# Three decode pairs of each attention computed between token tiles of the projections, and the second layer's projections reordered

## What is computed

```python
def diff_attention(q, k, v, lam, q_pos0):             # layer A
    ...
    p = jax.nn.softmax(jnp.where(mask, s, -jnp.inf), axis=-1)
    w = p[:, :, 0] - lam * p[:, :, 1]
    outs.append(jnp.einsum('bhqk,bkhd->bqhd', w.astype(v.dtype), vb))

def stick_breaking_attention(q, k, v, q_pos0):        # layer B
    ...
    log_1m = jnp.where(mask, jax.nn.log_sigmoid(-z), 0.0)
    suffix = lax.cumsum(log_1m, axis=3, reverse=True) - log_1m
    a = jnp.where(mask, jnp.exp(jax.nn.log_sigmoid(z) + suffix), 0.0)
    outs.append(jnp.einsum('bhqk,bkhd->bqhd', a.astype(v.dtype), vb))
```

## Time and profile before

| | |
|---|---|
| median of 3 runs | 1649.18 us (1644.54 to 1650.6) |
| span of the profiled execution | 1647.5 us |
| TensorE busy | 1616.3 us (98%) |
| VectorE busy | 1151.9 us (70%) |
| ScalarE (ACT) busy | 740.6 us (45%) |
| GpSimd (POOL) busy | 145.7 us (9%) |
| DMA | 265.45 MB, mean 161 GB/s |

### The profile page before, as it was taken

One profiled execution on the slowest core, in us unless ns is written; L12 is line 12 of the kernel. 1 busy time (PEld: TensorE's weight loads), 2 busy tenths in 40 slices (PEclk: granted clock), 3 DMA queues, 4 the chain that ended last, 5 costly groups with the idle time before them and its releaser, 6 DMA issues.

```text
span 1647.5 us, 31458 instructions
## 1 busy us (share of the span) xinstructions
PE 1616.3 (98%) x13140; PEld 1483.3 (90%) x13140; DVE 1151.9 (70%) x1605; ACT 740.6 (45%) x1228; POOL 145.7 (9%) x123
## 2 busy tenths in 40 slices
PE   8999999999999999999999999999999999999999
PEld 6888766699999999999999896666999999999999
DVE  5765477668984797488742328989689848974874
ACT  5444366765541344134432215768555413531441
POOL 0000000012210011012000000000122201110110
PEclk9999999999999999999999999999999999999999
DMA  7133899941222122222244358996412221221222
GB/s 286 52 111 132 350 418 418 419 160 52 86 94 103 52 78 103 77 78 78 103 166 140 112 209 360 420 418 288 167 66 89 95 85 52 103 102 53 78 103 90
DMA packets 39596, 265.45 MB, mean 161 GB/s; under 512 B 4256, under 2 KB 4640, under 8 KB 10272
## 3 DMA queue, kind: packets, MB, share of 16 engines
q1 hardware_dynamic: 36720, 252.95, 39.8%
q0 software_dynamic: 2736, 10.49, 1.8%
HBM read 247.69 MB, written 15.73 MB: 160 GB/s over the span
## 4 chain that ended last, share of the span: by engine, by line
PE 85%; DVE 8%; DMA 3%; issue 2%; ACT 2%; SPq 0%; DVEq 0%; ACTq 0%
PE ps L584 30%; PE ps L799 28%; PE ps L268 5%; PE ps L269 4%; PE ps L270 4%; PE ps L1260 2%; PE ps L1319 2%; DVE s_lo L748 2%; PE ps L611 2%; PE ps L1204 2%; DMA kv<-in_v_a 1%; PE ps L1238 1%; DMA xT<-in_v_a 1%; PE ps L1225 1%; DVE pw L1621 1%
## 5 line engine op out<-in xcount | busy, mean ns | idle before, releaser
L230 ACT ACTIVATE w_hi<-w_raw 128x2048 fp32r<-128x2048 f32 x55 | 105.1, 1910 | 190.3 <-PE ps L584 158.5
L246 DVE TENSOR_TENSOR w_lo<-w_raw,w_hi 128x2048 fp32r<-128x2048 f32 x55 | 126.0, 2291 | 71.4 <-ACT w_hi L230 71.4
L744 ACT ACTIVATE s_hi<-t 128x512 fp32r<-128x512 f32 x176 | 109.4, 626 | 144.6 <-PE ps L799 65.8
L799 PE MATMUL ps<-hs_hi,s_hi 128*128 128x320 f32 x528 | 163.8, 310 | 0.0
L799 PE MATMUL ps<-hs_hi,s_lo 128*128 128x320 f32 x528 | 163.2, 309 | 0.0
L799 PE MATMUL ps<-hs_lo,s_hi 128*128 128x320 f32 x528 | 163.1, 309 | 0.0
L584 PE MATMUL ps<-gu_hi,w_hi 128*128 128x320 f32 x692 | 157.9, 309 | 0.2
L584 PE MATMUL ps<-gu_lo,w_hi 128*128 128x320 f32 x692 | 157.7, 309 | 0.0
L584 PE MATMUL ps<-gu_hi,w_lo 128*128 128x320 f32 x692 | 157.6, 309 | 0.0
L748 DVE TENSOR_TENSOR s_lo<-t,s_hi 128x512 fp32r<-128x512 f32 x176 | 132.8, 760 | 5.4 <-ACT s_hi L744 4.6
L268 PE MATMUL ps<-w_hi,h_hi 128*128 128x512 f32 x320 | 126.8, 396 | 8.1 <-DVE h_lo L300 8.1
(11 more groups left out here) (298 smaller groups left out, 3995.9 us busy)
## 6 DMA issues: line engine op xcount, KB each, us to landing
w_raw<-in_w SPq DMA_DIRECT2D x99, 1024.0 KB, 4.8
kv<-in_k_a SPq DMA_DIRECT2D x12, 1024.0 KB, 16.1
kv<-in_v_a SPq DMA_DIRECT2D x12, 1024.0 KB, 16.7
kv<-in_v_s SPq DMA_DIRECT2D x12, 1024.0 KB, 12.6
kv<-in_k_s SPq DMA_DIRECT2D x12, 1024.0 KB, 15.0
xT<-in_k_a SPq DMA_DIRECT2D x8, 1024.0 KB, 17.4
xT<-in_k_s SPq DMA_DIRECT2D x8, 1024.0 KB, 11.7
work<-in_v_a SPq DMA_DIRECT2D x7, 1024.0 KB, 14.9
```

What stands on the lines that cost most here:

```text
L230: nc.scalar.activation(w_hi[s][:, :, :], w_raw[:, s, :, :], ACT.Copy).then_inc(hi_done, 1)
L246: nc.vector.tensor_tensor(w_lo[s][:, :, :], w_raw[:, s, :, :], w_hi[s][:, :, :].bitcast(F32), ALU.subtract).then_inc(lo_done, 1)
L744: nc.scalar.activation(s_hi[i][:, :, :], factor(j % 2, i), ACT.Copy).then_inc(hi_done, 1)
L799: last = nc.tensor.matmul(ps[:, bank[i], 0:HALF], w[:, p, :], m[:, p, :], start=(i < 3 and p == 0 and a == 0), stop=(p == 3 and a == 2), s ...
```

## The change

- `EARLY = 3`: the first three decode pairs of each attention, now sequences 0, 1, 2 with the first half of the heads (`PAIRS` sets the new order of the 16), are computed during the last two units before the slots, in fixed places after token tiles (`pe_early`, `act_early_before`, `act_early`), in banks 5 to 7, one pair after the other, with tiles of their own (`sp_early` in `rows`, `sw_early` in `extra`).
- The slots still number 16, with the same prompt steps; slot i now has pair i + 3, and slots 13, 14 and 15 have none.
- Layer B's units come in the order keys, queries, values, so that the last two units are token units there too. `h_lo` is made anew twice (`low_again`), for the queries in the keys' last unit and for the values in the queries' last unit.
- The ring's order differs: in A 16 pieces have places before the end of the units, in B 14; further loads of SP move among them. `qs` has room for four sequences and lies in `xT`.
- The norm of the decode outputs in layer A (`sub_pe(7)`, `sub_pe(8)`) moves into the last slot.

```diff
-        order = [("qkv", 12, TT, 1), ("oa", 4, 2, 1), *layer(0), ("ks", 4, 2, 1), ("vs", 4, TT, 1), ("qb", 4, 2, 1),
+        order = [("qkv", 12, TT, 1), ("oa", 4, 2, 1), *layer(0), ("ks", 4, 2, 1), ("qb", 4, 2, 1), ("vs", 4, TT, 1),
...
-        RING_A = ("x0 x1 extra work0 work1 raw1 w_hi0 w_lo0", "x0 x1 w_hi1 w_lo1 extra work0 work1 raw1 w_hi0 w_lo0")
-        RING_B = ("x0 x1 extra raw1 w_hi0 w_lo0", "x0 x1 work0 work1 w_hi1 w_lo1 extra raw1 w_hi0 w_lo0")
+        RING_A = ("x0 x1 extra work0 work1 x0 x1 raw1 extra work0 work1 x0 w_hi0 w_lo0 x1 raw1",
+                  "w_hi1 w_lo1 extra work0 work1 x0 w_hi0 w_lo0 x1 raw1")
+        RING_B = ("x0 x1 work0 work1 x0 x1 raw1 work0 work1 x0 x1 raw1 w_hi0 w_lo0",
+                  "w_hi1 w_lo1 extra work0 work1 x0 x1 raw1 w_hi0 w_lo0")
...
+        PAIRS = [(b, 0) for b in range(EARLY)] + [(b, 1) for b in range(EARLY)] + \
+            [(b, g) for b in range(EARLY, DEC_B) for g in range(G)]
...
+            def pe_early(self, unit, t):
+
+                step = (unit, t)
+                if step == (0, 0):
+                    self.pe_s(0)
+                elif step == (0, 2):
+                    self.pe_weights(0)
+                elif step == (0, 3):
+                    self.pe_new(1)
+                    self.pe_v(0)
+                    self.pe_s(1)
+                elif step == (1, 0):
+                    self.pe_o(0)
+                    self.pe_weights(1)
+                elif step == (1, 1):
+                    self.pe_new(2)
+                    self.pe_v(1)
+                    self.pe_s(2)
+                elif step == (1, 3):
+                    self.pe_o(1)
+                    self.pe_weights(2)
+                elif step == (1, 4):
+                    self.pe_ps(0)
+                    self.pe_s(3)
+                    self.pe_v(2)
...
             def pe_a(self, pe):
-                for n in range(N_PAIRS):
-                    k = 2 * n
+                for i in range(N_PAIRS):
+                    k, n = 2 * i, i + EARLY
...
+                    if n + 1 < N_PAIRS:
+                        self.pe_s(n + 1)
+                    if n < N_PAIRS:
+                        self.pe_v(n)
...
+        def low_again(dve, gain, hi, ph, free, done, made=None):
+
+            for t in range(KT):
+                if made is not None:
+                    dve.wait_ge(made, t + 1)
+                dve.wait_ge(*((free, t + 1) if t < KT - 1 else (mm, tiles_before(ph, 0))))
+                nc.vector.scalar_tensor_tensor(h_lo[:, t, :], xT[:, t, :], norms["kv"].g(t, gain),
+                                               hi[:, t, :].bitcast(F32), ALU.mult, ALU.subtract).then_inc(done, 1)
...
-            ta.loads(sp_, slice(3, 5), {"work0": [(qk["stored"], 64), (qk["tr"], 8)]})
+            work_free = [(qk["stored"], 64), (qk["tr"], 8)]
+            ta.loads(sp_, slice(3, 9), {"work0": work_free, "work1": work_free, "raw1": [(lo_done, splits[u_a - 1])]})
             load(u_a, 0)
-            ta.loads(sp_, slice(5, None), {"raw1": [(lo_done, splits[u_a - 1])],
+            ta.loads(sp_, slice(9, None), {"raw1": [(lo_done, splits[u_a - 1])],
                                            "w_hi0": [(mm, tiles_before("qkv", 11))],
                                            "w_hi1": [(mm, tiles_before("oa", 0))]})
...
+            x_free, work_free = [(kept, 16), (mix1["back"], KT)], [(mm, tiles_before("vs", 0))]
+            tb.loads(sp_, slice(0, 4), {"x0": x_free, "x1": x_free, "work0": work_free, "work1": work_free})
+            load(u_v + 3, 1)
+            tb.loads(sp_, slice(4, 9), {"raw1": [(lo_done, splits[u_b - 1])]})
+            load(u_b, 0)
+            tb.loads(sp_, slice(9, None), {"w_hi0": [(mm, tiles_before("vs", 3))],
+                                           "w_hi1": [(mm, tiles_before("ob", 0))],
+                                           "extra": [(tb.s["p"], EARLY)]})
...
             nc.scalar.preload_act_table_set("sigmoid_and_others")
-            tb.act_b(act, "ob", [(kq["stored"], 48)])
+            split_hi(act, "vs", 3, 1)
+            tb.act_early_before(act)
+            act.wait_ge(mm, tiles_before("vs", 3))
+            token_evac(act, "vs", 1, lambda t: v5[:, t, 2 * UC:4 * UC], kq["vev"], lambda t: tb.act_early(act, t))
+            tb.act_b(act, [(mm, tiles_before("ob", 0))], "ob", [(kq["stored"], 48)])
...
-            for j in range(2, 11):
+            for j in range(2, 10):
                 token_unit(pe, "qkv", j, qk["ev"])
-                if j < 10:
-                    qk_transposes(pe, j - 2)
+                qk_transposes(pe, j - 2)
             pe.wait_ge(qk["tev"], 8)
             pe.wait_ge(setup["const"], 1)
-            ta.pe_ps(0)
-            token_unit(pe, "qkv", 11, qk["ev"], between=lambda t: ta.pe_s(0) if t == 1 else None)
+            for j in range(2):
+                token_unit(pe, "qkv", 10 + j, qk["ev"], between=lambda t: ta.pe_early(j, t))
             ta.pe_a(pe)
```

More of the change, by code:

```diff
@@ L456, in first_unit, with token_unit @@
                         last.then_inc(mm, 1)
-        def token_unit(pe, ph, j, ev, free=None, k_done=None, between=None):
+        def token_unit(pe, ph, j, ev, free=None, ready=None, between=None):
             pe.wait_ge(lo_done, split_count(ph, j))
+            if ready is not None:
+                pe.wait_ge(*ready)
             for t in range(TT):
@@ L587, in feature_unit @@
                                 stop=(k == kts - 1 and i == 2), skip_group_check=True)
+                    if k_done is not None and n == 1 and k < kts - 1:
+                        last.then_inc(k_done, 1)
                 last.then_inc(mm, 1)
@@ L1262, in pe_s, with scored, pe_new @@
                     last.then_inc(s["kused"], 1)
-                if 1 not in part:
-                    return
+                if 1 in part and (n == 0 or n >= EARLY):
+                    self.pe_new(n).then_inc(s["s"], 1)
+            def scored(self, eng, n):
+                if 0 < n < EARLY:
+                    eng.wait_ge(self.s["kused"], 2 * n + 2)
+                else:
+                    eng.wait_ge(self.s["s"], 1 if n == 0 else n - EARLY + 2)
+            def pe_new(self, n):
+                pe, s = nc.tensor, self.s
+                b, g = PAIRS[n]
+                q = qs[:, b % 4]
+                pe.wait_ge(s["q"], b + 1)
+                self.wait(pe, s["x"], n)
                 self.wait(pe, s["wn"], n)
                 self.wait(pe, s["o"], n - 1)
+                if n == EARLY:
+                    self.tile_out(pe, 2)
                 for t in range(4):
@@ L1627, in dve_prod, with odd, dve_q @@
                 nc.vector.tensor_tensor(x, x, self.pw[p][:, :, SEQ - n + 1:SEQ + 1], ALU.mult).then_inc(s["pw"], 1)
-            def queries(self, n):
-                return n // G + (2 if self.b and n > 0 else 1)
-            def dve_q(self, b, tiles=slice(0, KT)):
+            def odd(self, n):
+                return sw_early if n < EARLY else sw
+            def dve_q(self, b):
                 s = self.s
-                self.wait(nc.vector, s["s"], 2 * b - 2)
+                if b >= 4:
+                    self.scored(nc.vector, PAIRS.index((b - 4, 1)))
                 new = slice(b * DEC_T, (b + 1) * DEC_T)
@@ L1766, in dve_b_begin, with dve_b @@
+            def dve_b(self, dve, ch, begin, ended, first, stored):
+                nc.vector.memset(sw_early[:, KEYS:KEYS + 4], 1.0)
+                for b in range(4):
+                    self.dve_q(b)
+                for n in range(EARLY):
+                    self.dve_sprod(ch, n)
+                    if n > 0:
+                        self.dve_o(n - 1)
+                    self.dve_wn(n)
+                for w in begin:
+                    dve.wait_ge(*w)
                 nc.vector.memset(pw0[:, :, SEQ:SEQ + 4], 1.0)
-                nc.vector.memset(sw[:, KEYS:KEYS + 4], 1.0)
@@ L1785, in dve_b @@
+                for w in ended:
+                    dve.wait_ge(*w)
+                ch.link(nc.vector.memset(pw1[:, :, SEQ:SEQ + 4], 1.0))
+                for i in range(N_PAIRS):
+                    k, n = 2 * i, i + EARLY
+                    if i % 2 == 1:
                         self.dve_pt(k - 1)
                     self.dve_prod(ch, k + 1, lambda: self.dve_new(n))
-                    if n % 2 == 0 and n + 2 < N_PAIRS:
-                        self.dve_q(n // 2 + 1)
+                    self.dve_next_q(n)
@@ L1800, in dve_b @@
                     dve.wait_ge(*w)
-                self.dve_lo(2)
-                self.dve_o(N_PAIRS - 1)
-                for t in range(3, 6):
+                for t in range(2, 5):
                     self.dve_lo(t)
@@ L1900, in kq_dve @@
                 for n in range(2):
-                    if j == 3 and n == 1 and between is not None:
+                    if j == 3 and n == 1:
                         between()
```

586 lines of the change are left out of this document (320 added, 266 removed).

## The result

The changed kernel takes 1700.3 us (median of four runs, 1697.5 to 1700.7) against 1648.7 before: a ratio of 1.031, interval 1.030 to 1.033. It is 51.6 us slower; 36 were forecast, and the time lies 3 us above the range. The profiled execution has a span of 1698.3 us.

What follows compares the result with a forecast made beforehand. TensorE bounds the projections, loads the end of each attention's pairs, then prompt steps run alone. 1647.5 + 19 (first attention) + 17 (second) = 1683.5 profiled, so 1685 us as median; range 1664 to 1697.

Steps and rivals of the forecast that it cites:

- Added to the units: Units before the slots: a pair costs TensorE 5.3 us; units end at 202.3 in A, near 1014.7 in B.
- The three waits: TensorE in the last units: 1.6 us for copies and 1.8 for query layout in A, 4.0 for it in B.
- the query wait: Second attention, before scores 0: TensorE waits 4.0 us for the query layout that VectorE makes.
- When the loads end: Key and value loads end at 330.4 in A and 1150.3 in B; last value products near 333 and at 1151.7.
- (1): Rival, chance 0.13: loads are not the limit, both stages end by their chains, +10 us each, 1669 us.
- the main case: Forecast, chance 0.72: loads set when each attention's last value products end, the slots without pairs follow; 1685 us.
- the one from 1150.3 to 1151.7: Second attention: loads end at 1150.3, and the last value products follow at 1151.7.
- The tails: From last value products to output product, with slots lacking a pair: 24 us in A, 23 us in B.
- rival (2): Chance 0.06: TensorE's clock falls to half in the three slots without a pair, 6 us on each stage, 1697 us.
- A slot without a pair: Attention slots with prompt steps only: in A 7.0 us against 9.0 with a pair, set by the steps' chain.
- (3): Rival, chance 0.05: slots run at VectorE's busy time, 6.7 us a slot in A, 1639 us.
- (4): Rival, chance 0.04: prompt-only slots take 4.7 us and loads run ahead, 1649 us.

## Why the prediction was right in direction and short in size

**Added to the units: right.** Units ended at 200.6 in A (202.3 forecast, of which 1.1 is that this trace runs 1.1 us earlier at unit 10), and in B 190.1 us after the first unit of the keys, with 189.2 forecast. The three waits were right within 0.4 us. The pieces, not costed inside the units, made TensorE wait 0.9 us in B, and up to 2.5 in other runs. Behind the query wait the clock took another 1.5 us that the sum did not have.

**When the loads end: right in A.** Last value products at 332.4, forecast 333. The forecast that slots can't run ahead of the loads was the right one of (1) and the main case: half the bytes gave 12.5 us back in A.

**When the loads end: right in B too, but the slots did not end with them.** The last value products came 6.2 us later than forecast, beyond the 0.9 of the units. The failed step is the one from 1150.3 to 1151.7: the loads alone gave the first figure and VectorE's slots alone an earlier end, so I took the later of two sums and set the last products right behind the last piece. The trace runs 23.1 us late at the keys' first unit, so the loads were forecast to end at 1173.4. They did, or somewhat before:

```profile
1165.00:1170.00 5.00, 5.00 (x48) 3.42 (x52) 4.93 (x5) 4.44 (x9) 0.00 (x0) 1.00 1.01 421
1170.00:1175.00 5.00, 4.72 (x120) 3.46 (x112) 4.89 (x9) 3.16 (x6) 0.00 (x0) 1.00 0.67 241
```

The last value products ended at 1181.9, and none waited for a piece behind 1140. A slot took 138.9 / 13 = 10.7 us on the average; with half the bytes 9.85 (128.1 / 13). Of these 10.8 us 5.9 lie in the first two slots behind the units (27.4 against 21.5 us from pair 2's new tokens' products to pair 4's), where TensorE waits for pieces up to 2.7 us at a time, and 4.9 in the other eleven. From the end of the units the slots need 132.5 us with half the bytes, the loads 135.6 by my sum, and both together took 143.3: early waits were not made good by later slots that have hardly any slack of their own. In A of the kernel before I had the same mixture and missed it: its slots were 9.0 at first and 9.9 to 10.0 from the tenth on, and that kernel got 9 us faster with half the bytes.

**The tails: too short**, 24 for 29.7 and 23 for 26.7. My sum had the minima, exponentials, combinations and the split (2.3 us there, 2.0 as measured). It left out what else stands in the engines' queues: in A the norm that the change itself had moved (1.8 us) and the single bank of the transposes (0.3 at most); with 2.2 for the clock that explains 4.3 of the 5.7 us. The other 1.4, and at least 2.0 of B's 3.7, stay open; neither the split nor the copies were tried in B. The fall of the clock was rival (2), at 6 us a stage and 0.06, and stood in the sum at nothing. It came: 2.2 us in A's tail, at most 1.7 in B's, 1.5 behind the query wait. Its chance was far too low: the prediction says itself that no stretch of the trace was so empty, so the 1.00 of its rows was no evidence against it.

**A slot without a pair: right in A at full clock, too cheap with the clock that it got.** I had 7.0 us against 9.0. Spread among full ones it takes 7.0 in A where the clock stayed at 1.00, and 8.3 to 8.5 in the three places where it fell. So in A the change pays 5.3 us a pair in a full TensorE and got back about half a microsecond at most places, 2.0 at best. In B it gets 3.6, and pays with the later loads.

**The rivals.** (1) fell (the loads limit, 25 us). (2) held as a mechanism with about a third of its price in the tails. (3) and (4) fell: no slot ran at VectorE's busy time, even with half the bytes.

Put together: 19 + 17 = 36 forecast; A came to 23.9 (its tail), B to 27.4 (0.9 more in the units, 6.2 in the slots, 3.7 in the tail, less 0.4 of rounding in the forecast's 17), and 0.9 came back between A's output product and the keys: 50.4.

## What to carry to other kernels

Work moved from a stage that is paced by latencies into one where TensorE is full costs its whole duration there, and saves only what it had in the chain it left: measure that by an empty slot, not by its busy time, and read the granted clock of that slot beside its length. Put units without work of their own kind among the others and not at the end, where nothing hides them and the clock falls. Where two limits lie within some per cent of each other, halve one of them in an experiment before you take the later of two sums, and ask which waits at the start of the stage can still be made good at its end.

## What was not expected of the hardware

With a wait of 3.99 us in an otherwise full TensorE the granted clock was 0.84 and 0.82 in the two stretches of five microseconds from 995, and 16 scores took 2.74 us instead of 1.92; this wait cost 1.5 us more than its length. In a slot whose longest wait of TensorE is 2.32 us the clock fell in one kernel and not in another, with the same work behind that wait, and 8.20 us became 9.50; why it fell in one alone is not shown. And a filler that keeps the clock at 1.00 earned only 2.2 us in a tail of 29.7 where TensorE is busy 20.5 us: most of that chain, as I read it, is on the other engines.
